# Modulating the two k-tiles of a pair on two engines, with a longer first piece of the split ahead and the masks cast in FFN 0

## The chip, the core and the metric

The kernel runs on one core of one Trainium2 chip. The core has five engines that each take their own queue of instructions in order and meet only through semaphores: TensorE (PE; its weight loads are shown as PEld), VectorE (DVE), ScalarE (ACT), GpSimd (POOL) and SyncE (SP), the last two issuing loads here. The metric is the device time of one launch in microseconds.

## What is computed

Two decoder layers over 256 tokens of width 1024, each with a half-step SwiGLU FFN, a token mixer and another FFN, every one modulated by shift, scale and gate rows computed from `c`, and closed by a residual with a LayerNorm. The reference, cut to what matters:

```python
D_MODEL = 1024; SEQ = 256; DEPTH = 2; N_HEADS = 8; D_FF = 2816
...
def layer_norm(x, g, b):
    xf = x.astype(jnp.float32)
    mu = jnp.mean(xf, axis=-1, keepdims=True)
    var = jnp.mean(jnp.square(xf - mu), axis=-1, keepdims=True)
    return ((xf - mu) * lax.rsqrt(var + LN_EPS) * g.astype(jnp.float32) + b.astype(jnp.float32)).astype(x.dtype)

def modulate(x, shift, scale):
    return x * (1.0 + scale[:, None, :]) + shift[:, None, :]

def post_norm_residual(x, y, gate, weight, g, b):
    return layer_norm(DEEPNORM_ALPHA * x + weight * (1.0 + gate[:, None, :]) * y, g, b)

def swiglu(h, w_in, w_out):
    g, u = jnp.split(h @ w_in, 2, axis=-1)
    return (jax.nn.silu(g) * u) @ w_out
...
    cond = jax.nn.silu(c)
...
    for l in range(DEPTH):
        if l == N_A_LAYERS:
            kv_mod = (cond @ w_kv_ada + b_kv_ada).reshape(b, 2, d)
            kv = modulate(x, kv_mod[:, 0], kv_mod[:, 1]) @ w_kv_b
...
        mod = (cond @ w_ada[l] + b_ada[l]).reshape(b, 3 * N_SUB, d)
        h = modulate(x, mod[:, 0], mod[:, 1])
        x = post_norm_residual(x, swiglu(h, w_ffn_in[l, 0], w_ffn_out[l, 0]), mod[:, 2], 0.5, ln_g[l, 0], ln_b[l, 0])
        h = modulate(x, mod[:, 3], mod[:, 4])
        if l < N_A_LAYERS:
            q, k, v = jnp.split(h @ w_qkv_a[l], 3, axis=-1)
...
            y = moba_attention(q, k, split_heads(v))
        else:
            q = split_heads(h @ w_q_b[l - N_A_LAYERS])
            y = stick_breaking_attention(q, k_sh, v_sh)
        y = merge_heads(y) @ w_o[l]
        x = post_norm_residual(x, y, mod[:, 5], 1.0, ln_g[l, 1], ln_b[l, 1])
        h = modulate(x, mod[:, 6], mod[:, 7])
        x = post_norm_residual(x, swiglu(h, w_ffn_in[l, 1], w_ffn_out[l, 1]), mod[:, 8], 0.5, ln_g[l, 2], ln_b[l, 2])
    return x
```

## The kernel before

All matrix products are done in three parts: a float32 weight `w` is split into `w_hi` (the value rounded to fp32r) and `w_lo = w - w_hi`, the activations likewise, and TensorE adds `hi*hi`, `lo*hi` and `hi*lo` into PSUM (lines 1460 to 1462 and 1556 to 1558 are the three matmuls of 128x512). Weights stream through five raw slots in chunks of 128 x 2048 elements (1 MB). SyncE loads a chunk (line 409), ScalarE writes `w_hi` (`split_hi`, line 586 for a whole chunk, 594 and 597 for one in two pieces), VectorE writes `w_lo` (`split_lo`, line 979) and with it frees the raw slot.

The tokens are two tiles of 128 (t = 0, 1), the width is eight k-tiles of 128 (k = 0 to 7). The order of all work on each engine is written out by hand; nothing is scheduled. Work runs as FFN 0, norm 0, projection and attention of layer 0, norm 1, FFN 1, norm 2, the shared keys and values (`KV_PAIRS`), FFN 2, norm 3, the queries of layer 1 (`Q_PAIRS`), stick-breaking attention, norm 4, FFN 3, last norm. After each of norms 0 to 4 stands the following input `h` in transposed form. What happens in one norm, for i = 0 to 4:

- VectorE (`norm`, line 1215): the residual of tile 0 in two halves (lines 1171, 1172), mean, normalising (1201); the first half of tile 1's residual; then `h_tile` of tile 0; then the second half of tile 1's residual, its mean and normalising; then `h_tile` of tile 1.
- ScalarE (`norm`, line 728): squares with sums (711) and the standard deviation (725) of tile 0; `h_tile` of tile 0; the first square of tile 1; the first 1024 columns of the split of the chunk ahead (594); the second square of tile 1, which waits for VectorE's residual; the deviation; a table load (739); `h_tile` of tile 1; the rest of the split (597).
- TensorE transposes the normalised tile in eight products (`turn_normed`, 1482). For tile 1 it does so inside `lead`, line 1588: 18 matmuls of tile 0 come first (k-tiles 0 to 5), then the eight transposes, then k-tiles 6 and 7, then tile 1 from k-tile 0 on.

`h_tile` works in halves of four k-tiles, each half in two pairs. A transposed k-tile lies in PSUM; modulating it (times `coef` scale, plus `coef` shift) gives `h_full` for tile 0 or `tmp` for tile 1; from it ScalarE writes `hT_hi` of a pair (697) and VectorE `hT_lo` of the pair (1151). In a half ScalarE modulates the first pair (691) and VectorE the second (1143). `h_hi` of the first pair waits for ScalarE's own semaphore `h_act`, that of the second for `h_dve`:

```python
def h_hi(i, t, pair):
    act.wait_ge(h_dve if pair % 2 else h_act, modulated(i, t, pair // 2))
```

`turn_place` says in which PSUM bank a transposed k-tile lies: the two tiles of a pair share a bank, so ScalarE and VectorE read from two different banks. The input of FFN 0 (i = 0) is made in the same way at the start, half by half, with the splits of chunks 1 and 2 after the first halves; that of FFN 2 (i = 4) is made among the projections of keys and values.

The three masks (identity, causal, strict) are cast to bf16 on VectorE (1322) just after norm 0 and used by the attention's scores. `quarter` inside `ffn` multiplies rows of `w_ada` by elements of the condition (1018, 1027) to make the modulation rows of later stages.

## Time and profile before

| | us |
|---|---|
| median of 3 runs | 1035.16 |
| lowest, highest of them | 1034.12, 1035.77 |
| the profiled execution | 1035.72 |
| its span | 1033.9 |
| TensorE busy | 1010.2 (98%) |
| VectorE busy | 788.1 (76%) |
| ScalarE busy | 529.3 (51%) |

The span reaches from the first to the last instruction of the profiled execution. The page's idle column puts down each idle stretch to the one that released it. A TensorE weight load is issued one matmul ahead, and matmul ends are modelled, so a stop of TensorE is best read from the starts of its matmuls, which stand 0.23 us apart at full clock.

### The profile page before, as it was taken

How to read it: one execution, taken by the hardware profiler on the slowest of the kernel's cores; microseconds unless marked ns; L12 is line 12 of the kernel's file. 1: busy time of each engine (PE TensorE's matmuls, PEld its weight loads, DVE VectorE, ACT ScalarE, POOL GpSimd, SP SyncE). 2: the span in 40 equal slices, each digit the busy share in tenths (PEclk: the TensorE clock that was granted, in tenths of full speed). 3: DMA queues.
4: the chain of work that ended last, by engine and by line, in shares of the span. 5: the costliest groups of instructions: out<-in, count | busy, mean ns of one | idle time of the engine just before them, and what ended most of it. 6: DMA issues, size and time to landing. Idle time of an engine off the chain costs nothing.

```text
span 1033.9 us, 12560 instructions
## 1 busy us (share of the span) xinstructions
PE 1010.2 (98%) x4768; PEld 834.0 (81%) x4768; DVE 788.1 (76%) x962; ACT 529.3 (51%) x872; POOL 86.0 (8%) x160
## 2 busy tenths in 40 slices
PE   4999999999999999999999999999999999999997
PEld 3878888887888888888888888888888888888885
DVE  6887677889877897768887587677888987545486
ACT  1635453566565753544474645453568764434433
POOL 0011111001000011112000011111001010000000
PEclk9999999999999999999999999999999999999999
DMA  9999999956785399899928499999846748556541
GB/s 353 376 380 359 303 299 313 320 163 203 255 274 163 129 377 346 294 315 305 332 101 295 142 358 301 308 304 311 302 161 207 242 141 306 185 183 204 174 151 41
DMA packets 147492, 265.63 MB, mean 257 GB/s; under 512 B 8424, under 2 KB 98920, under 8 KB 147432
## 3 DMA queue, kind: packets, MB, share of 16 engines
q1 hardware_dynamic: 124448, 182.87, 51.7%
q0 software_dynamic: 20928, 75.53, 20.9%
q10 hardware_dynamic: 2056, 6.42, 2.1%
q8 instruction: 38, 0.62, 0.2%
q14 instruction: 22, 0.18, 0.1%
HBM read 263.75 MB, written 1.05 MB: 256 GB/s over the span
## 4 chain that ended last, share of the span: by engine, by line
PE 89%; DVE 5%; ACT 2%; DMA 2%; issue 2%; SPq 0%; DVEq 0%; ACTq 0%
PE psum L1460 18%; PE psum L1462 18%; PE psum L1461 17%; PE psum L1556 9%; PE psum L1558 9%; PE psum L1557 9%; PE psum L1595 2%; DMA raw<-in_w_ffn_in 2%; DVE w_lo L979 2%; PE psum L1495 1%; ACT w_hi L586 1%; DVE tmp L1000 1%; PE psum L1861 1%; PE psum L1482 1%; PE psum L1692 1%
## 5 line engine op out<-in xcount | busy, mean ns | idle before, releaser
L979 DVE TENSOR_TENSOR w_lo<-raw,w_hi 128x2048 fp32r<-128x2048 f32 x164 | 371.6, 2287 | 61.7 <-ACT w_hi L586 59.5
L1460 PE MATMUL psum<-w_hi,hT_hi 128*128 128x512 f32 x896 | 355.9, 397 | 0.7 <-DVE w_lo L979 0.2
L1462 PE MATMUL psum<-w_hi,hT_lo 128*128 128x512 f32 x896 | 350.0, 391 | 0.0
L1461 PE MATMUL psum<-w_lo,hT_hi 128*128 128x512 f32 x896 | 349.0, 390 | 0.0
L586 ACT ACTIVATE w_hi<-raw 128x2048 fp32r<-128x2048 f32 x159 | 299.8, 1915 | 11.0 <-DMA raw<-in_w_ffn_in 9.5
L604 ACT ACTIVATE tmp<-psum 128x256 f32<-128x256 f32 x88 | 33.6, 383 | 338.3 <-PE psum L1462 338.3
L1460 PEld LDWEIGHTS psum<-w_hi,hT_hi 128*128 128x128 f32 x896 | 168.2, 188 | 36.7 <-issue 2.4
L1462 PEld LDWEIGHTS psum<-w_hi,hT_lo 128*128 128x128 f32 x896 | 168.2, 188 | 35.9
L1461 PEld LDWEIGHTS psum<-w_lo,hT_hi 128*128 128x128 f32 x896 | 168.5, 188 | 33.0
L1556 PE MATMUL psum<-w_hi,a_hi 128*128 128x512 f32 x368 | 148.5, 404 | 0.0
L1558 PE MATMUL psum<-w_hi,a_lo 128*128 128x512 f32 x368 | 144.3, 392 | 0.0
L1557 PE MATMUL psum<-w_lo,a_hi 128*128 128x512 f32 x368 | 144.2, 392 | 0.0
L1067 DVE TENSOR_TENSOR tmp<-psum,tmp 128x256 f32<-128x256 f32 x88 | 37.3, 424 | 119.7 <-ACT tmp L604 118.6
L1027 DVE SCALAR_TENSOR_TENSOR acc<-qT,cond,acc 128x1024 f32<-128x1024 f32 x64 | 82.0, 1281 | 3.3
L1027 DVE SCALAR_TENSOR_TENSOR acc<-ada,cond,acc 128x1024 f32<-128x1024 f32 x62 | 79.5, 1283 | 5.8 <-DMA ada<-in_w_ada 1.0
L1558 PEld LDWEIGHTS psum<-w_hi,a_lo 128*128 128x128 f32 x368 | 69.5, 189 | 15.0
L1557 PEld LDWEIGHTS psum<-w_lo,a_hi 128*128 128x128 f32 x368 | 69.7, 189 | 13.1
L1556 PEld LDWEIGHTS psum<-w_hi,a_hi 128*128 128x128 f32 x368 | 69.5, 189 | 13.3 <-issue 0.2
L507 POOL DMA_DIRECT2D ada<-in_w_ada x72 | 38.3, 532 | 410.4 <-DVE acc L1027 279.4
L507 POOL DMA_DIRECT2D qT<-in_w_ada x56 | 29.5, 528 | 292.4 <-DVE acc L1027 234.3
L1071 DVE TENSOR_TENSOR a_lo<-psum,a_hi 128x256 fp32r<-128x256 f32 x84 | 35.1, 418 | 7.3 <-ACT a_hi L608 7.3
L608 ACT ACTIVATE a_hi<-psum 128x256 fp32r<-128x256 f32 x84 | 31.9, 379 | 10.6 <-PE psum L1595 10.6
(171 smaller groups left out, 798.9 us busy)
## 6 DMA issues: line engine op xcount, KB each, us to landing
raw<-in_w_ffn_in SPq DMA_DIRECT2D x176, 512.0 KB, 5.6
raw<-in_w_ffn_out SPq DMA_DIRECT2D x88, 512.0 KB, 6.1
ada<-in_w_ada POOLq DMA_DIRECT2D x72, 512.0 KB, 6.1
qT<-in_w_ada POOLq DMA_DIRECT2D x56, 512.0 KB, 5.1
raw<-in_w_qkv_a SPq DMA_DIRECT2D x24, 512.0 KB, 4.7
raw<-in_w_o SPq DMA_DIRECT2D x16, 512.0 KB, 4.6
raw<-in_w_kv_b SPq DMA_DIRECT2D x16, 512.0 KB, 5.2
raw<-in_w_ada SPq DMA_DIRECT2D x4, 1024.0 KB, 16.3
```

Of the source, the lines that this page charges most:

```text
L507: pool.dma_start(ada_rows[place], ada_view(w)[:, row, j * D:(j + 1) * D])\
L586: nc.scalar.activation(hi_of(n), slot_of(n), ACT.Copy).then_inc(w_hi_ready, 1)
L979: nc.vector.tensor_tensor(lo_of(n), slot_of(n), hi_of(n).bitcast(F32), ALU.subtract)\
L1027: nc.vector.scalar_tensor_tensor(out=acc[:, :], in0=part, scalar=factor, in1=base, op0=ALU.mult, op1=ALU.add).then_inc(acc_steps, 1)
L1067: nc.vector.tensor_tensor(a_full[t], step_bank(f, s, t)[:, 256:512], silu_t[t], ALU.mult).then_inc(a_ready, 1)
L1071: nc.vector.tensor_tensor(inner_part(s, t, 1), inner_bank(f, s, t), inner_part(s, t, 0).bitcast(F32), ALU.subtract).then_inc(a_lo_ready, 1)
L1460: nc.tensor.matmul(dst, s_hi, m_hi, start=start, stop=False)
L1461: nc.tensor.matmul(dst, s_hi, m_lo, start=False, stop=False)
L1462: return nc.tensor.matmul(dst, s_lo, m_hi, start=False, stop=stop)
L1556: nc.tensor.matmul(dst, hi, m[0], start=first and j == 0, stop=False)
L1557: nc.tensor.matmul(dst, hi, m[1], start=False, stop=False)
L1558: end = nc.tensor.matmul(dst, lo, m[0], start=False, stop=last and j == 1)
```

## The change

1. A pair is modulated by both engines at once: ScalarE takes its even k-tile, VectorE its odd one, each with a semaphore step per tile. `h_hi` waits for both. ScalarE goes modulate, `h_hi`, modulate, `h_hi`; VectorE does its two tiles of a half, then `h_lo` of both pairs. `turn_place` puts the two tiles of a pair into two banks.
2. The first piece of the chunk ahead, which stands in front of the second square, has 1408 columns (`AHEAD`) in place of 1024.
3. In norms 0, 2 and 3 the rest of that split, 640 columns, is moved out of the norm to behind the copy of the first projected tile; in norms 1 and 4 it stays behind `h_tile`.
4. The masks are cast in FFN 0, after the last `split_lo` of step 4.

```diff
+AHEAD = 1408
...
+        def tiles_modulated(i, t, pair):
+
+            return 2 * modulated(i, t, pair // 2) - 1 + pair % 2
...
-            pair = k // 2
             if i in (0, 4):
-                bank, at = y[2 * (1 - t) + pair % 2], (k % 2 + 2 * (pair // 2)) * P
+                bank, at = y[2 * (1 - t) + k % 2], k // 2 * P
             else:
-                bank, at = ((misc + y[0:2]) if t == 0 else (y[2:4] + misc))[pair], (k % 2) * P
+                bank, at = ((misc + y[0:2]) if t == 0 else (y[2:4] + misc))[2 * (k // 4) + k % 2], (k % 4 // 2) * P
             return bank[:, at:at + P]
...
-            def h_pair(i, t, half):
-
-                act.wait_ge(turned, turned_count(i, t, half))
-                act.wait_ge(coef_ready, coef_count(i, half))
-                for k in (4 * half, 4 * half + 1):
-                    last = nc.scalar.activation(h_fulls[t][:, k, :], turn_place(i, t, k),
-                                                ACT.Identity, scale=coef[:, i, 0, k:k + 1], bias=coef[:, i, 1, k:k + 1])
-                last.then_inc(h_act, 1)
+            def modulate(i, t, pair):
+
+                act.wait_ge(turned, turned_count(i, t, pair // 2))
+                act.wait_ge(coef_ready, coef_count(i, pair // 2))
+                k = 2 * pair
+                nc.scalar.activation(h_fulls[t][:, k, :], turn_place(i, t, k), ACT.Identity,
+                                     scale=coef[:, i, 0, k:k + 1], bias=coef[:, i, 1, k:k + 1]).then_inc(h_act, 1)
 
             def h_hi(i, t, pair):
-                act.wait_ge(h_dve if pair % 2 else h_act, modulated(i, t, pair // 2))
+                act.wait_ge(h_act, tiles_modulated(i, t, pair))
+                act.wait_ge(h_dve, tiles_modulated(i, t, pair))
                 nc.scalar.activation(hT_hi[:, 2 * pair:2 * pair + 2, t * P:(t + 1) * P],
                                      h_fulls[t][:, 2 * pair:2 * pair + 2, :], ACT.Copy).then_inc(h_hi_ready, 1)
 
             def h_half(i, t, half):
-                h_pair(i, t, half)
-                h_hi(i, t, 2 * half)
-                h_hi(i, t, 2 * half + 1)
+                for pair in (2 * half, 2 * half + 1):
+                    modulate(i, t, pair)
+                    h_hi(i, t, pair)
...
                 deviation(i, 0)
                 h_tile(h, 0)
                 first_square(i, 1)
-                split_hi_first(ahead, CH // 2)
+                split_hi_first(ahead, AHEAD)
                 deviation(i, 1)
...
                 h_tile(h, 1)
-                split_hi_rest(ahead, CH // 2)
+                if i in (1, 4):
+                    split_hi_rest(ahead, AHEAD)
...
             keep_tile(q0, 0)
+            split_hi_rest(n + 2, AHEAD)
             split_hi(n + 3)
...
             keep_values(v0, 0, 0)
+            split_hi_rest(n + 2, AHEAD)
             split_hi(n + 3)
...
-            h_pair(4, 1, 0)
-            h_pair(4, 1, 1)
+            for pair in range(4):
+                modulate(4, 1, pair)
...
             keep_tile(q0, 0)
+            split_hi_rest(n + 2, AHEAD)
             split_hi(n + 3)
...
                     split_lo(n + 3 * s + 4)
+                    if (f, s) == (0, 4):
+                        dve.wait_ge(cst_in, 32)
+                        for m, mask in enumerate((ident, causal, strict)):
+                            last = nc.vector.tensor_copy(masks[:, m, :], mask)
+                        last.then_inc(masks_ready, 1)
...
-            def h_pair(i, t, half):
-
-                dve.wait_ge(turned, turned_count(i, t, half))
-                dve.wait_ge(coef_ready, coef_count(i, half))
-                for k in (4 * half + 2, 4 * half + 3):
-                    last = nc.vector.tensor_scalar(h_fulls[t][:, k, :], turn_place(i, t, k),
-                                                   coef[:, i, 0, k:k + 1], coef[:, i, 1, k:k + 1], ALU.mult, ALU.add)
-                last.then_inc(h_dve, 1)
+            def modulate(i, t, pair):
+
+                dve.wait_ge(turned, turned_count(i, t, pair // 2))
+                dve.wait_ge(coef_ready, coef_count(i, pair // 2))
+                k = 2 * pair + 1
+                nc.vector.tensor_scalar(h_fulls[t][:, k, :], turn_place(i, t, k), coef[:, i, 0, k:k + 1],
+                                        coef[:, i, 1, k:k + 1], ALU.mult, ALU.add).then_inc(h_dve, 1)
...
             def h_half(i, t, half):
-                h_pair(i, t, half)
+                modulate(i, t, 2 * half)
+                modulate(i, t, 2 * half + 1)
                 h_lo(i, t, 2 * half)
                 h_lo(i, t, 2 * half + 1)
...
             gate_unit = GATE_OF[1]
-            dve.wait_ge(cst_in, 32)
-            for m, mask in enumerate((ident, causal, strict)):
-                last = nc.vector.tensor_copy(masks[:, m, :], mask)
-            last.then_inc(masks_ready, 1)
             rope(q0, 0)
...
-            for half in range(2):
-                h_pair(4, 1, half)
+            for pair in range(4):
+                modulate(4, 1, pair)
```

Two places as the queues have them, and a third for the masks. First ScalarE in norm 0, from the start of `h_tile` of tile 0 to the second square of tile 1, before:

```order
L691 ACTIVATE h_full<-psum,coef 128x128 [waits coef_ready,turned]
L691 ACTIVATE h_full<-psum,coef 128x128
L697 ACTIVATE hT_hi<-h_full 128x2x128 [waits h_act]
L697 ACTIVATE hT_hi<-h_full 128x2x128 [waits h_dve]
...
L711 ACTIVATE psum,sq<-qT,first_mean 128x512 [waits first_mean_ready]
L594 ACTIVATE w_hi<-raw 128x1024 [waits w_used,raw_in0]
L711 ACTIVATE psum,sq<-qT,first_mean 128x512 [waits z_ends]
```

and after:

```order
L695 ACTIVATE h_full<-psum,coef 128x128 [waits coef_ready,turned]
L701 ACTIVATE hT_hi<-h_full 128x2x128 [waits h_dve,h_act]
L695 ACTIVATE h_full<-psum,coef 128x128 [waits coef_ready,turned]
L701 ACTIVATE hT_hi<-h_full 128x2x128 [waits h_dve,h_act]
...
L715 ACTIVATE psum,sq<-qT,first_mean 128x512 [waits first_mean_ready]
L598 ACTIVATE w_hi<-raw 128x1408 [waits w_used,raw_in0]
L715 ACTIVATE psum,sq<-qT,first_mean 128x512 [waits z_ends]
```

The first split of the half moved ahead of the second modulated tile, and each split waits for a tile of VectorE as well as for one of its own. The second half, left out in both, reads the same as the first.

Next ScalarE at the end of norm 3 and the start of the queries (`h_full` in L753 and L758 is the copy of the first projected tile), before:

```order
L697 ACTIVATE hT_hi<-tmp 128x2x128 [waits h_dve]
L597 ACTIVATE w_hi<-raw 128x1024
L753 ACTIVATE h_full<-psum 128x512 [waits first_tile]
L586 ACTIVATE w_hi<-raw 128x2048 [waits w_used,raw_in1]
L753 ACTIVATE h_full<-psum 128x512 [waits w_used]
```

and after:

```order
L701 ACTIVATE hT_hi<-tmp 128x2x128 [waits h_dve,h_act]
L758 ACTIVATE h_full<-psum 128x512 [waits first_tile]
L601 ACTIVATE w_hi<-raw 128x640
L590 ACTIVATE w_hi<-raw 128x2048 [waits w_used,raw_in1]
L758 ACTIVATE h_full<-psum 128x512 [waits w_used]
```

The copy moved ahead of the rest of the split.

Last VectorE in FFN 0, step 4 to 5, after the change; the two splits follow each other directly before it:

```order
L1035 SCALAR_TENSOR_TENSOR acc<-ada,cond,acc 128x1024 [waits acc_steps,ada_in1]
L987 TENSOR_TENSOR w_lo<-raw,w_hi 128x2048 [waits w_hi_ready]
L1135 CAST masks<-cst 128x128 [waits cst_in]
L1135 CAST masks<-cst 128x128 x2
L987 TENSOR_TENSOR w_lo<-raw,w_hi 128x2048 [waits w_hi_ready]
L1075 TENSOR_TENSOR tmp<-psum,tmp 128x256 [waits silu_ready]
```

The casts moved here from behind norm 0.

## Rows read from the trace of the kernel before

**Rows 1.** The page: TensorE's busy time, share of the span, number of instructions

```profile
PE 1010.2 (98%) x4768; PEld 834.0 (81%) x4768; DVE 788.1 (76%) x962; ACT 529.3 (51%) x872; POOL 86.0 (8%) x160
```

**Rows 2.** Waits of the weight loads: us in total, times, longest us

```profile
PEld psum L1460 <- issue: 2.4, 5, 0.5
PEld psum L1460 <- DVE w_lo L979: 1.2, 2, 0.7
```

**Rows 3.** Timeline of ScalarE in norm 0: start us, length us, engine, line, operation

```profile
226.25 0.81 ACT L691 ACTIVATE h_full<-psum,coef 128x128 f32<-128x128 f32 x2 [2.17 <-PE psum L1482]
...
230.11 1.04 ACT L594 ACTIVATE w_hi<-raw 128x1024 fp32r<-128x1024 f32 x1
231.56 0.69 ACT L711 ACTIVATE psum<-qT,first_mean 128x512 f32<-128x512 f32 x1 [0.41 <-DVE qT L1172]
...
234.63 0.81 ACT L691 ACTIVATE tmp<-psum,coef 128x128 f32<-128x128 f32 x2 [0.62 <-PE psum L1482]
235.47 0.73 ACT L697 ACTIVATE hT_hi<-tmp 128x256 fp32r<-128x256 f32 x2
```

**Rows 4.** Timeline of VectorE in norm 0

```profile
226.77 0.73 DVE L1143 TENSOR_SCALAR h_full<-psum,coef 128x128 f32<-128x128 f32 x2
...
230.10 0.69 DVE L1171 TENSOR_TENSOR qT<-psum,gate 128x512 f32<-128x512 f32 x1
...
232.94 1.00 DVE L1201 TENSOR_SCALAR qT<-qT,nmean,rstd 128x512 f32<-128x512 f32 x2
234.63 0.73 DVE L1143 TENSOR_SCALAR tmp<-psum,coef 128x128 f32<-128x128 f32 x2 [0.69 <-PE psum L1482]
235.92 0.76 DVE L1151 TENSOR_TENSOR hT_lo<-tmp,hT_hi 128x256 fp32r<-128x256 f32 x2 [0.56 <-ACT hT_hi L697]
```

**Rows 5.** Timeline of TensorE in norm 0 and the projection behind it

```profile
233.99 1.04 PE L1482 MATMUL psum<-cst,qT 128*128 128x128 f32 x8
...
235.79 0.39 PE L1461 MATMUL psum<-w_lo,hT_hi 128*128 128x512 f32 x1
236.02 0.40 PE L1462 MATMUL psum<-w_hi,hT_lo 128*128 128x512 f32 x1
236.49 0.48 PE L1460 MATMUL psum<-w_hi,hT_hi 128*128 128x512 f32 x1
...
245.72 0.50 PE L1460 MATMUL psum<-w_hi,hT_hi 128*128 128x512 f32 x1 [0.25 <-DVE w_lo L979]
```

**Rows 6.** Timeline of three engines at the start of the queries

```profile
778.85 1.05 ACT L597 ACTIVATE w_hi<-raw 128x1024 fp32r<-128x1024 f32 x1
779.80 0.58 ACT L753 ACTIVATE h_full<-psum 128x512 f32<-128x512 f32 x1
779.92 2.29 DVE L979 TENSOR_TENSOR w_lo<-raw,w_hi 128x2048 fp32r<-128x2048 f32 x1 [0.53 <-ACT w_hi L597]
780.27 1.90 ACT L586 ACTIVATE w_hi<-raw 128x2048 fp32r<-128x2048 f32 x1
...
784.72 2.29 DVE L979 TENSOR_TENSOR w_lo<-raw,w_hi 128x2048 fp32r<-128x2048 f32 x1
...
787.06 0.49 PE L1460 MATMUL psum<-w_hi,hT_hi 128*128 128x512 f32 x1
```

**Rows 7.** Timeline of VectorE in FFN 0, and the casts after norm 0

```profile
125.65 0.42 DVE L1067 TENSOR_TENSOR tmp<-psum,tmp 128x256 f32<-128x256 f32 x1 [2.37 <-ACT tmp L604]
...
238.15 0.49 DVE L1322 CAST masks<-cst 128x128 bf16<-128x128 f32 x3
```

**Rows 8.** The chain of work that ended last, at the start: start us, us, what

```profile
40.83 13.66 DMA raw<-in_w_ffn_in
```

**Rows 9.** Timeline of TensorE in FFN 0: its idle before this transpose

```profile
59.74 0.44 PE L1595 MATMUL psum<-cst,tmp 128*128 128x128 f32 x2 [1.85 <-DVE tmp L1067]
```

**Rows 10.** Windows: us, busy (count) of PE, PEld, DVE, ACT, POOL; granted clock, DMA, GB/s

```profile
60.00:62.00 2.00, 2.00 (x7) 1.49 (x6) 2.00 (x5) 1.79 (x2) 0.00 (x0) 0.56 1.10 349
62.00:64.00 2.00, 2.00 (x7) 1.57 (x6) 2.00 (x2) 0.89 (x2) 0.00 (x0) 0.59 1.11 349
```

## The prediction

> **What bounds the kernel now.** First the page: TensorE (PE) is busy 1010.2 of 1033.9 us [rows 1], so another engine matters only where TensorE waits for it. Next the waits of its weight loads [rows 2]: after the start there are only five stops before a matmul of line 1460, 2.4 us in sum, and two stops for `w_lo`, 1.2 us in sum. These rows overstate the loss, since a weight load goes one matmul ahead. What is lost shows in the starts: two matmuls in a row start 0.23 us apart (235.79, 236.02), the next one 0.47 us later, at 236.49 [rows 5]. So a stop costs 0.24 us and five cost 1.2 us. They stand where the second token tile of each norm reaches TensorE; the matmul needs the first pair of `hT_lo`, which VectorE works on from 235.92 and ends at about 236.35 [rows 4]. The two `w_lo` stops cost less than their 1.2 us, some 0.7. All that the norms and what follows them can give back is thus about 1.9 us, 0.18%. A measurement of this kernel can tell about 0.2%, 2.1 us, from no change.
>
> **Part 1: the pairs, second tile.** Both engines start at 234.63 [rows 3, 4]. Before, ScalarE modulates k-tiles 0 and 1 in 0.81 us (two of 0.45 with 0.1 of overlap) and starts `hT_hi` of pair 0 at 235.47 [rows 3]. After, ScalarE does k-tile 0 while VectorE does k-tile 1, so `hT_hi` starts at 235.11, 0.36 us earlier, and `hT_lo` of the pair ends at 236.0. The stop of 0.24 us would go: five norms, -1.2 us.
>
> **Part 2: the pairs, first tile.** Here the two don't start together: ScalarE at 226.25 [rows 3], VectorE at 226.77 [rows 4], because the residual of the second tile's first half stands ahead of it. Before, only the second `hT_hi` of a half needs VectorE. After, every one does, and VectorE still makes `hT_lo` of pairs 0 and 1 ahead of its k-tiles 5 and 7. So pair 2 goes round both engines: `hT_hi` 1, `hT_lo` 1, k-tile 5, `hT_hi` 2. I stepped both queues with the rows' durations (modulate 0.45 and 0.41, split 0.42 and 0.43, 0.03 us from an end to the start of what needs it, 0.1 us of overlap where nothing is needed). So stepped, the old order gives the trace's times within 0.05 us. The new order lets VectorE go on to the last residual at 230.8, where it starts at 230.10 now [rows 4]: 0.7 us later.
>
> **Part 3: 1408 columns.** 1024 columns take 1.04 us, and ScalarE then idles 0.41 us until the residual is done [rows 3]; 2048 take 1.90 us [rows 6]. A column costs 0.84 ns, so 1408 take 1.37 us. By part 2 ScalarE starts this piece 0.8 us late and is free at 232.33, the residual ends at 232.24: the longer piece itself costs 0.1 us. Second square, standard deviation and normalising are then 0.77 us late. TensorE begins the transposes at 233.99 [rows 5] and needs only the first half of the normalised tile, ready at about 233.5 (the two halves run from 232.94 to 233.94) [rows 4]: 0.5 us of room. Of 0.77 us, 0.3 is left as a new stop ahead of the transposes. In norms 1 and 4, where VectorE starts its first tile later still against ScalarE, the stepping gives 0.66 late and 0.2 of stop. With the transposes later the second tile's `hT_lo` lands at its old time, and TensorE, later too, doesn't wait for it. So the stop moves: parts 1 to 3 together give 0.3 - 0.24, about +0.1 us for norms 0, 2 and 3 and 0 for norms 1 and 4.
>
> **Part 4: where the rest of the split stands.** The second tile lasts 0.6 us longer on both engines (each pair is again a chain over both) and starts 0.3 us later, so ScalarE is through with it 0.9 us later. In norms 1 and 4 the rest of the split shrinks from 1.05 us [rows 6] to 0.72 (640 columns) and stays where it is; `w_lo` and the gated product behind it come 0.5 us late, within TensorE's room there: 0. In the others a tile copy of 0.58 us [rows 6] now stands ahead of the rest.
> - Norm 0: the copy starts when it did, RoPE follows it and not the rest, and both `w_lo` keep their times. The stop before 245.72 [rows 5] stays and swallows this norm's 0.1 us: 0.
> - Norm 2 (keys and values): `w_lo` 1.0 us late, with about that much room. From 0 to 0.3; I take 0.15, and with the norm's own 0.1: +0.25.
> - Norm 3 (queries): VectorE runs without a break from `w_lo` at 779.92 over two gate products to the second `w_lo`, 784.72 to 787.0, and TensorE starts at 787.06 behind it [rows 6]. That stretch begins when the rest ends, 778.85 + 1.05 = 779.9. Now ScalarE is free at 779.7, copies until 780.3 and ends the rest at 780.92. All moves by 1.03 us, with TensorE waiting for its end: **+1.05 us**, this norm's own stop included.
>
> **Part 5: the masks.** The three casts, 0.49 us, leave the projection, where they lay beside the wait for a tile copy, for FFN 0, where VectorE idles 2.37 us before its next gated product [rows 7]: 0 and 0.
>
> **Part 6: the start.** In the first half tiles the chain over both engines costs ScalarE 0.6 us, so `w_lo` of chunks 1 and 2, and the load that the first frees, come about 0.55 us later. That load takes 13.66 us from issue to landing [rows 8], which is a queue and not its own transfer. TensorE has 1.85 us of idle behind it [rows 9]. I take 0 and keep 0.55 for the range.
>
> **Sum.** 0 + 0 + 0.25 + 1.05 + 0 = +1.3 us. On the profiled execution (1035.72 us, of which 1033.9 are its span) that gives 1037.0; it lay 0.56 us above the median of the runs shown, so against the median 1036.4.
>
> **The rivals.**
> - *The room before the transposes hides the first tile.* If the first tile's lateness stays under 0.5 us, nothing stops the transposes and part 1's 0.24 us stands in norms 1, 2 and 4 (norm 0's goes into its `w_lo` wait): -0.7. If the queries' stretch, too, isn't later, their norm's 0.24 us goes as well: -1.0, 1034.2. With that stretch late by 0.9 the sum is +0.2, 1035.4. For it: the room is real. Against: VectorE starts half a microsecond after ScalarE, by the program's order. Chance 0.12 for 1034.2 and 0.13 for 1035.4.
> - *The half clock at the start (the slower side).* The granted clock is 0.56 in the 2 us from 60 and 0.59 in the next 2 [rows 10], right behind TensorE's 1.85 us of idle [rows 9]; before and after it is full. At half clock (1.2 GHz for 2.4) this loses 2 x 0.44 + 2 x 0.41 = 1.7 us. The later chunks 1 and 2 make a break or two in TensorE's work shortly before. If these or a longer idle bring a second such stretch, 1036.4 + 1.7 = 1038.1; it decides from where chunk 1 or 2 comes later than TensorE's room, about 0.3 us for chunk 1. Chance 0.13. A shorter idle without the stretch would give 1034.7: 0.05.
>  The Trainium skill (TensorE: Matmul & The Clock Gate, What's actually happening) says that the gate is released by activity and that its phase is independent of the program's start. The trace agrees on the first; no row shows the second.
> - *The load follows its issue.* The 0.55 us of part 6 reach TensorE: 1037.0. Chance 0.07.
> - *The change does more than remove stops.* Above 0.2% needs the start's idle to shrink besides all the norms' stops: 1032.9. Chance 0.05.
>
> The forecast as worked out has the remaining 0.45.
>
> **How the numbers follow.** Likeliest: 1036.4. 1034.2 less a few tenths for the spread of three runs gives the low end, 1033.9; the high end, 1038.0, stands just short of the clock's 1038.1 and holds the queue's 1037.0 and norm 2's 0.15. Left out are the gain of 0.05 and most of the clock's 0.13. Within 0.2% is 1033.1 to 1037.2. Slower by more: the clock's 0.13 and a part of the forecast's upper side, 0.19. Faster by more: 0.07. The rest is 0.74.
>
> **What would show it.** Right: the second tile's first matmul 0.23 us behind the one ahead; a stop of 0.2 to 0.3 us before the transposes of the second tile; the second square some 0.75 us later against the first tile's start; the queries' second `w_lo` about 1 us later against the matmuls of their norm, and TensorE right behind it. Wrong: `hT_hi` of the first tile's first pairs not held by VectorE, transposes without a stop, or a queries' stretch that starts no later.

## The result, and the profile after

The changed kernel takes 1037.38 us (median of 9 runs, 1036.96 to 1039.46) where the kernel before, run beside it, takes 1034.12 us (9 runs, 1033.85 to 1035.77): slower by 3.3 us (the medians' quotient is 1.0032; the recorded ratio is 1.0026, with 1.0017 to 1.0035 as its interval). The forecast was 1036.4 us, 1.3 us slower, with 1033.9 to 1038.0 as the range. So the time lay in the range, but the likeliest case had been "within 0.2%", and the loss is two and a half times the one worked out (about twice by the recorded ratio). The profiled execution of after took 1037.43 us, 1035.6 of which are its span.

The executions of the kernel before, here and in the batches below, fall into two groups, at 1033.8 to 1034.7 and 1035.1 to 1036.5 us; two of the three that the prediction had lie in the upper one, and so does its profile (1035.72 us).

The page of after has the same busy times as [rows 1] within 0.2 us on TensorE and VectorE; all of the loss is waiting:

```profile
PE 1010.1 (98%) x4768; PEld 832.2 (80%) x4768; DVE 788.2 (76%) x962; ACT 529.5 (51%) x872; POOL 85.2 (8%) x160
```

The waits of its weight loads answer [rows 2] (us in total, times, longest us). L1469 is the matmul that was L1460, L1491 the transposes of a norm (1482 before), L1604 the transposes of an FFN's product (1595 before):

```profile
PEld psum L1491 <- DVE qT L1214: 3.2, 5, 0.7
...
PEld psum L1469 <- DVE w_lo L987: 3.0, 3, 1.2
PEld psum L1469 <- issue: 1.4, 3, 0.5
PEld psum L1604 <- DVE tmp L1075: 1.4, 3, 0.8
```

Five waits before the transposes are new, the two for `w_lo` have become three, and the five short ones of the second tiles are gone; the three short ones here stand elsewhere (at 41 us, in the keys and values at 544, in the queries at 784). Norm 0 shows the first. ScalarE, against [rows 3]:

```profile
224.85 0.46 ACT L695 ACTIVATE h_full<-psum,coef 128x128 f32<-128x128 f32 x1 [2.21 <-PE psum L1491]
225.82 0.42 ACT L701 ACTIVATE hT_hi<-h_full 128x256 fp32r<-128x256 f32 x1 [0.52 <-DVE h_full L1156]
...
227.91 0.42 ACT L701 ACTIVATE hT_hi<-h_full 128x256 fp32r<-128x256 f32 x1 [0.53 <-DVE h_full L1156]
...
229.74 1.37 ACT L598 ACTIVATE w_hi<-raw 128x1408 fp32r<-128x1408 f32 x1
231.01 0.66 ACT L715 ACTIVATE psum<-qT,first_mean 128x512 f32<-128x512 f32 x1
```

VectorE, against [rows 4]:

```profile
225.32 0.73 DVE L1156 TENSOR_SCALAR h_full<-psum,coef 128x128 f32<-128x128 f32 x2
226.27 0.43 DVE L1163 TENSOR_TENSOR hT_lo<-h_full,hT_hi 128x256 fp32r<-128x256 f32 x1 [0.23 <-ACT hT_hi L701]
...
229.50 0.68 DVE L1184 TENSOR_TENSOR qT<-psum,gate 128x512 f32<-128x512 f32 x1
...
232.37 1.02 DVE L1214 TENSOR_SCALAR qT<-qT,nmean,rstd 128x512 f32<-128x512 f32 x2
```

TensorE, against [rows 5]:

```profile
232.37 0.39 PE L1471 MATMUL psum<-w_hi,hT_lo 128*128 128x512 f32 x1
232.97 1.13 PE L1491 MATMUL psum<-cst,qT 128*128 128x128 f32 x8 [0.21 <-DVE qT L1214]
233.85 0.47 PE L1469 MATMUL psum<-w_hi,hT_hi 128*128 128x512 f32 x1
...
235.08 0.40 PE L1471 MATMUL psum<-w_hi,hT_lo 128*128 128x512 f32 x1
235.32 0.39 PE L1469 MATMUL psum<-w_hi,hT_hi 128*128 128x512 f32 x1
```

Read in this order: ScalarE waits 0.52 and 0.53 us for VectorE's k-tile before two of its four `hT_hi`; its second square starts 6.16 us after its first modulate (224.85 to 231.01) where it was 5.31 us (226.25 to 231.56); VectorE normalises 7.52 us after that modulate (6.69 before); and TensorE's transposes start 0.60 us behind the matmul ahead of them, where matmuls in a row are 0.23 apart. The stop of the second tile is gone: 235.08 to 235.32 is 0.24 us, where [rows 5] has 0.47.

To see where the 3.2 us arise, each matmul of after was set against the same matmul of before in the two profiled executions, since TensorE runs the same 4768 in the same order. The shift (start in after less start in before) moves almost only in steps; a few hundredths of drift between two steps are counted with the nearer one:

| place | what makes the step | step, us | predicted |
|---|---|---|---|
| start and FFN 0, up to 59.9 | +0.17 before 31, stops of +0.30 at 41 and +0.91 at 47 (chunks 1 and 2 late), then 1.26 less idle at 59.9 | +0.17 | 0 |
| norm 0 | transposes +0.45, second tile -0.32 | +0.14 | +0.1, swallowed later |
| attention, 287 | one transposition late | +0.15 | 0 |
| norm 1 | the same two | +0.13 | 0 |
| FFN 1, 352 and 363 | first transposes +0.10, the next ones +0.54 | +0.64 | 0 |
| norm 2 | the same two | +0.20 | +0.1 |
| keys and values, 544 | `w_lo` later | +0.33 | +0.15 |
| norm 3 | the same two | +0.16 | in the next line |
| queries, 784 and 788.5 | `w_lo` +0.37, second `w_lo` +0.75 | +1.12 | +1.05 |
| norm 4 and FFN 3 | the same two +0.08, first transposes +0.10 | +0.18 | 0 |
| sum | | +3.2 | +1.3 |

The two spans differ by only 1.7 us, since before's profiled execution also lost 1.6 us at half clock [rows 10], and after's has none there (last section).

The largest step that the prediction did not have is at 363 in FFN 1. VectorE and then TensorE of after there:

```profile
348.38 2.29 DVE L987 TENSOR_TENSOR w_lo<-raw,w_hi 128x2048 fp32r<-128x2048 f32 x1 [0.20 <-ACT w_hi L601]
...
362.52 0.42 DVE L1075 TENSOR_TENSOR tmp<-psum,tmp 128x256 f32<-128x256 f32 x1
```

```profile
362.30 0.39 PE L1471 MATMUL psum<-w_hi,hT_lo 128*128 128x512 f32 x1
363.08 0.41 PE L1604 MATMUL psum<-cst,tmp 128*128 128x128 f32 x2 [0.40 <-DVE tmp L1075]
```

And TensorE of before at the same transposes:

```profile
363.15 0.39 PE L1462 MATMUL psum<-w_hi,hT_lo 128*128 128x512 f32 x1
363.42 0.41 PE L1595 MATMUL psum<-cst,tmp 128*128 128x128 f32 x2
```

From the first `w_lo` behind norm 1 VectorE has no idle time for 14.5 us, until the product that these transposes need. Nor had it any in before, where the same row reads:

```profile
348.71 2.29 DVE L979 TENSOR_TENSOR w_lo<-raw,w_hi 128x2048 fp32r<-128x2048 f32 x1 [0.53 <-ACT w_hi L597]
...
362.86 0.42 DVE L1067 TENSOR_TENSOR tmp<-psum,tmp 128x256 f32<-128x256 f32 x1
```

There it ended just in time (at 363.28, and 0.27 us lie between the starts of matmul and transposes). That `w_lo` starts 0.33 us earlier in after (348.38 against 348.71), but the matmuls are 0.88 us earlier by then, so it is 0.55 us late against TensorE, and nearly all of the 0.55 arrives 14 us later.

The queries, against [rows 6]: ScalarE, VectorE, TensorE of after.

```profile
779.85 0.42 ACT L701 ACTIVATE hT_hi<-tmp 128x256 fp32r<-128x256 f32 x1
780.17 0.58 ACT L758 ACTIVATE h_full<-psum 128x512 f32<-128x512 f32 x1
780.65 0.73 ACT L601 ACTIVATE w_hi<-raw 128x640 fp32r<-128x640 f32 x1
```

```profile
781.41 2.29 DVE L987 TENSOR_TENSOR w_lo<-raw,w_hi 128x2048 fp32r<-128x2048 f32 x1 [0.69 <-ACT w_hi L601]
...
786.20 2.29 DVE L987 TENSOR_TENSOR w_lo<-raw,w_hi 128x2048 fp32r<-128x2048 f32 x1
```

```profile
787.33 0.40 PE L1471 MATMUL psum<-w_hi,hT_lo 128*128 128x512 f32 x1
788.54 0.49 PE L1469 MATMUL psum<-w_hi,hT_hi 128*128 128x512 f32 x1 [0.81 <-DVE w_lo L987]
```

The stretch on VectorE starts 1.49 us later than the 779.92 of before (0.20 of it is the shift that after had by then), and TensorE starts 788.54 right behind its end. This is the part that went as forecast.

### The profile page after: what moved, and what is told of

Same layout as the page of the kernel before. It is cut to its first block, busy times and chain, and to the rows that moved or that the text cites. A ratio compares the mean times of both kernels' runs of the same rounds, so it can differ in the third digit from the quotient of the medians.

```text
span 1035.6 us, 12672 instructions
## 1 busy us (share of the span) xinstructions
PE 1010.1 (98%) x4768; PEld 832.2 (80%) x4768; DVE 788.2 (76%) x962; ACT 529.5 (51%) x872; POOL 85.2 (8%) x160
## 3 DMA queue, kind: packets, MB, share of 16 engines
HBM read 263.75 MB, written 1.05 MB: 256 GB/s over the span
## 4 chain that ended last, share of the span: by engine, by line
PE 80%; DVE 10%; ACT 5%; issue 3%; DMA 2%; SPq 0%; DVEq 0%; ACTq 0%
PE psum L1469 16%; PE psum L1471 16%; PE psum L1470 16%; PE psum L1565 8%; PE psum L1567 8%; PE psum L1566 8%; DVE w_lo L987 3%; DMA raw<-in_w_ffn_in 2%; PE psum L1604 2%; ACT w_hi L590 2%; PE psum L1504 1%; ACT psum L715 1%; DVE tmp L1008 1%; DVE qT L1185 1%; PE psum L1870 1%
## 5 line engine op out<-in xcount | busy, mean ns | idle before, releaser
L1469 PE MATMUL psum<-w_hi,hT_hi 128*128 128x512 f32 x896 | 356.0, 397 | 2.0 <-DVE w_lo L987 1.7
L1469 PEld LDWEIGHTS psum<-w_hi,hT_hi 128*128 128x128 f32 x896 | 168.2, 188 | 38.0 <-DVE w_lo L987 3.0
```

Source lines behind the costliest of these rows:

```text
L1469: nc.tensor.matmul(dst, s_hi, m_hi, start=start, stop=False)
```

## The experiments

Three batches, each against the kernel before on the same chip: its medians there were 1034.13, 1034.37 and 1034.54 us (27, 33 and 27 runs). The ratios are against those. "Against after" compares with 1037.38, which was measured in none of these batches. Kernels with the same start differ by up to 0.4 us at 59.9 us of their profiles, so differences of 0.3 us in the times stand for nothing; the steps inside a profile are read finer.

### The pairs alone, and everything but the pairs

`e1_pairs_only`: before, with the new pairs everywhere; 1024 columns, the rest in every norm, the masks as they were.

```
-AHEAD = 1408
+AHEAD = 1024
-                if i in (1, 4):
+                if i in (0, 1, 2, 3, 4):
                     split_hi_rest(ahead, AHEAD)
```

(The edit is shown against after; left out of it are the three later `split_hi_rest`, which are gone, and the masks, which are back.)

> The kernel before with the new pairs alone (both engines on each pair, in every tile); 1024 columns ahead, the rest of the split at the end of each norm, masks after norm 0. Theory (the first tile's chain over both engines makes the second tile late): transposes of the second tile stop TensorE by 0.2 to 0.3 us in each norm, the stop before the second tile's first matmul is gone, ScalarE leaves the norm 0.9 us late with a rest of 1.05 us behind it, so the stop in FFN 1 and the one at the queries' second chunk are there as well: +2.5 to +3.3 us against before. Rival (the longer piece and the moved rest do the harm, the pairs alone gain): -1 to +0.5 us.

1038.19 us, ratio 1.0038 (1.0025 to 1.005): +4.1 us, more than the 2.5 to 3.3 expected. Its profile has the expected steps before the transposes, in FFN 1 and in the queries, and one that was not expected, +0.93 against before, in the first projection:

```profile
241.82 0.47 PE L1465 MATMUL psum<-w_hi,hT_hi 128*128 128x512 f32 x1 [0.77 <-DVE w_lo L984]
```

The `w_lo` there stands behind RoPE (the rotation of queries and keys) on VectorE, and RoPE behind ScalarE's copy, which in this kernel waits for the rest of the split. `e2_all_but_pairs` keeps the other parts and has the old `h_pair` and `turn_place`:

```
-                for pair in (2 * half, 2 * half + 1):
-                    modulate(i, t, pair)
-                    h_hi(i, t, pair)
+                h_pair(i, t, half)
+                h_hi(i, t, 2 * half)
+                h_hi(i, t, 2 * half + 1)
```

> The changed kernel with the old pairs (each engine its own pair of a half): 1408 columns ahead, rest of the split behind the first projected copy in norms 0, 2 and 3, masks in FFN 0. Theory: ScalarE idles 0.41 us before the second square, 384 columns more cost 0.33 us of it, and the copy ahead of the rest costs the queries 0.16 us: 0 to +0.3 us against before, the five stops before the second tile as before. Rival (the longer piece and the moved rest do the harm): +2 us or more.

1033.5 us, 0.9994 (0.9985 to 1.0003): -0.6 us where 0 to +0.3 was expected; the interval holds 1. So the pairs are the whole loss and more, and the columns, the place of the rest and the masks give back a little (e1 to after: -0.8; before to e2: -0.6). In e2 the five stops at the second tiles are as before, and the `w_lo` stop of [rows 5] at 245.72 is gone (a step of -0.52): that is the gain of the rest behind the copy. A second step, -0.25 before the transposes of `acc` at 380, isn't explained by any run; in the queries e2 loses 0.15.

### Which pairs

`e3_second_tile_only` has the new pairs only in the second tile of each norm, with 1408 columns, the rest in every norm and the masks as in after. Shown is the condition alone; the old `h_pair` and `turn_place`, which hold wherever it is false, are left out here and in the variants below:

```
+        def both(i, t, half):
+            return t == 1 and i not in (0, 4)
```

> New pairs in the second tile of each norm alone, old pairs in the first tile and at the start; 1408 columns ahead, the rest of the split inside every norm, masks in FFN 0. Theory: the first tile ends on time, so the transposes don't stop and the five stops of 0.24 us go; ScalarE is 0.6 us longer in the second tile, 0.33 of it given back by the shorter rest, so the queries' stretch is 0.3 us late: -1.0 to -0.2 us against before. Rival (the waits between the engines cost as much in the second tile): 0 to +1 us.

1034.97 us, 1.0008 (0.9999 to 1.0017): +0.8, where I had expected a gain of 0.2 to 1.0; the rival named there (0 to +1) fits. Its profile has neither the transposes' stop nor the second tile's. It has others, behind the second tile; TensorE at the first one:

```profile
239.87 0.40 PE L1512 MATMUL psum<-w_hi,hT_lo 128*128 128x512 f32 x1
240.10 0.60 PE L1726 MATMUL psum<-cst,h_full 128*128 128x128 f32 x4
241.21 0.47 PE L1510 MATMUL psum<-w_hi,hT_hi 128*128 128x512 f32 x1 [0.51 <-DVE w_lo L1013]
```

Against before this is a step of +0.67, with +0.50 at 362.54 and +0.64 at 786.22: each time a `w_lo` or a product at the end of an unbroken row on VectorE that began with the end of the second tile. The chain over both engines makes the second tile longer, and that is paid behind the norm, in three places. Only the first half needs to be quick, so `e4_first_half_of_second_tile` has the new pairs in half 0 alone:

```
-            return t == 1 and i not in (0, 4)
+            return t == 1 and half == 0 and i not in (0, 4)
```

> As the kernel with new pairs in the second tile alone, but only in its first half (pairs 0 and 1); its second half and the first tile have the old pairs. Theory: the first hT_lo comes 0.36 us earlier as TensorE wants it, and ScalarE leaves the tile only 0.15 us later, less than the 0.33 us that the shorter rest gives back: the five stops go, the stop at the queries' second chunk shrinks by 0.1 to 0.2 us: -1.5 to -0.9 us against before, the fastest of the four. Rival: as fast as the kernel with the whole second tile.

1033.07 us, 0.9989 (0.998 to 0.9998): -1.1 us. In its profile all five stops of the second tile are gone, in steps of -0.32 or -0.33 (sum -1.6), and the three places of e3 are late again, but only by +0.13, +0.14 and +0.13 (at 242.51, 363.29 and 786.37). The net is that of part 1 of the prediction, priced there at -1.2; it agrees because a larger gain and a cost that part 1 did not have nearly make up for each other.

### The first tile

`e6_vector_modulates_first`: after, but in tile 0 of each norm VectorE does its four k-tiles before any `hT_lo`.

```
+                if t == 0 and i not in (0, 4):
+                    for pair in range(4):
+                        modulate(i, t, pair)
+                    for pair in range(4):
+                        h_lo(i, t, pair)
+                    return
```

> The changed kernel, but in the first tile of each norm VectorE modulates all its four k-tiles before it makes any hT_lo. Theory (pair 2 goes round both engines): ScalarE waits for VectorE at the first pair alone, the second square comes 0.35 to 0.4 us earlier, and of the lateness less than the 0.5 us of room is left, so the stops before the transposes go or fall under 0.1 us: -1.0 to -1.5 us against the changed kernel, +1.8 to +2.3 against before. Rival (the lateness is that of the first pair, or of the 1408 columns): -0.3 to 0 against the changed kernel.

1035.19 us, 1.0007 (0.9998 to 1.0015): -2.2 us against after, more than the 1.0 to 1.5 expected. VectorE, ScalarE and TensorE in norm 0:

```profile
225.22 1.36 DVE L1156 TENSOR_SCALAR h_full<-psum,coef 128x128 f32<-128x128 f32 x4
```

```profile
229.14 1.37 ACT L598 ACTIVATE w_hi<-raw 128x1408 fp32r<-128x1408 f32 x1
230.41 0.67 ACT L715 ACTIVATE psum<-qT,first_mean 128x512 f32<-128x512 f32 x1
```

```profile
232.21 0.39 PE L1477 MATMUL psum<-w_hi,hT_lo 128*128 128x512 f32 x1
232.44 1.06 PE L1497 MATMUL psum<-cst,qT 128*128 128x128 f32 x8
```

The second square comes 5.70 us after the first modulate (224.71), and all five stops before the transposes are gone, each step between -0.40 and -0.52, in sum -2.3 (its start gives another 0.15 and a few hundredths come back between the norms). So the round over both engines (`hT_hi` 1, `hT_lo` 1, k-tile 5, `hT_hi` 2) is what made the first tile late enough to stop TensorE: with `hT_lo` out of it and the pairs unchanged, 0.46 of the second square's 0.85 us go, and the 0.39 that is left stops nothing. The stops behind the second tile stay, at 543, 362 and 786.70 us.

### The columns and the rest

`e12_1024_columns` is after with `AHEAD = 1024`.

> The changed kernel with 1024 columns ahead in place of 1408, all else as changed. Theory (the longer piece costs the second square 0.1 us at most and spares 0.33 us behind the norms): stops before the transposes 0.1 us shorter, the stop in FFN 1 and those for w_lo behind norms 2 and 3 up to 0.33 us longer: +0.2 to +0.8 us against the changed kernel, +3.5 to +4.1 against before. Rival (the 1408 columns make the second square late): -1 us against the changed kernel.

1038.48 us, 1.004 (1.0028 to 1.0053): +1.1 us against after, a little over the upper end of what was expected (0.8), and +3.9 against before, within it. ScalarE in norm 0, and TensorE in FFN 1:

```profile
229.41 1.04 ACT L598 ACTIVATE w_hi<-raw 128x1024 fp32r<-128x1024 f32 x1
230.62 0.69 ACT L715 ACTIVATE psum<-qT,first_mean 128x512 f32<-128x512 f32 x1 [0.17 <-DVE qT L1185]
```

```profile
351.12 0.44 PE L1604 MATMUL psum<-cst,tmp 128*128 128x128 f32 x2 [0.19 <-DVE tmp L1075]
```

With 1024 columns the second square comes 6.15 us after the first modulate (224.47), with 1408 6.16: the first waits 0.17 us for VectorE's residual, the second starts behind the split with no wait, and the split and the residual end within 0.2 us of each other (231.11 and 230.92 in after). So in norm 0 the longer piece costs nothing ahead of the transposes. In the other norms it costs a little: the starts of matmul and transposes are 0.03, 0.10, 0.04 and 0.03 us farther apart in after than here. Its worth lies behind the norm, where the rest is 0.73 us and not 1.04: the profile of 1024 has steps of +0.18 at 241, +0.33 at 351, +0.33 at 544, +0.34 at 784 and +0.30 at 853 against after.

`e7_rest_in_norm` is after with the rest in every norm:

```
-                if i in (1, 4):
+                if i in (0, 1, 2, 3, 4):
```

> The changed kernel with the rest of the split (640 columns) inside every norm, ahead of the copy of the first projected tile. Theory: the queries' stretch starts 0.5 us earlier (-0.5), keys and values -0.2, but in norm 0 copy and RoPE and with them the w_lo behind them come 0.6 us later (+0.6): -0.3 to +0.1 us against the changed kernel, the three parts to be seen one by one in the trace. Rival (the copy ahead of the rest causes the queries' stop): -1.0 us, the stop at the queries' second chunk gone.

1036.99 us, 1.0022 (1.0013 to 1.0031): -0.4 against after, at the edge of what was expected; its start alone makes up as much (its profile is 0.40 us ahead at 59.9). Inside, the move of the rest shows with both signs: without it a stop of +0.64 appears at 241.47 (the first projection's `w_lo`, as in e3), while 0.35 at 544, 0.37 at 784 and 0.15 at 788 go. Moving the rest behind the copy pays 0.64 us in norm 0 and costs 0.35 and 0.52 in norms 2 and 3.

### The queries' row of VectorE

`e8_splits_first_in_queries`: after, both `w_lo` ahead of the gate products.

```
             split_lo(n + 2)
-            accumulate(gate_unit, 0)
             split_lo(n + 3)
+            accumulate(gate_unit, 0)
```

> The changed kernel with one line moved: in the queries VectorE makes both w_lo before the two gate products. Theory: the stop before the queries' second chunk, 0.98 us by the starts, is VectorE's unbroken stretch; with 2.6 us of products out of it the stop is gone: -0.8 to -1.0 us against the changed kernel. Rival (the stop is given back in the attention, whose queues are late anyway): -0.2 to 0 us.

1036.73 us, 1.0021 (1.0012 to 1.003): -0.65 against after, between the theory (-0.8 to -1.0) and the rival (-0.2 to 0); some 0.2 of it is this profile's start. VectorE, and TensorE at the first scores:

```profile
781.22 4.49 DVE L987 TENSOR_TENSOR w_lo<-raw,w_hi 128x2048 fp32r<-128x2048 f32 x2 [0.69 <-ACT w_hi L601]
```

```profile
790.61 0.70 PE L1859 MATMUL psum<-qT,kT 128*128 128x256 f32 x2 [0.35 <-ACT qT L762]
```

TensorE gains 1.1 us at 788.5, and loses 0.6 again at the scores, which wait for ScalarE's `qT`; the likely reason is that the products now stand ahead of the row that the queries' scaling needs, which no run separates. Half of the stop was order; the other half is not got rid of by order, since VectorE begins as late as before the edit (781.22 here, 781.41 in after, 0.2 of it the start).

### The start

`e5_start_only`: before, with the new pairs only in the first transposed input.

```
+        def both(i, t, half):
+            return i == 0
```

> The kernel before with the new pairs in the first FFN's input alone. Theory (the start costs little by itself): ScalarE's start is 0.55 us longer, TensorE stops for chunks 1 and 2 by up to 1 us in sum, and the idle before the transposes of FFN 0 shrinks by as much, so 0 to +0.3 us against before among executions of the same clock; since the long idle is broken up, fewer executions have the half-clock stretch of 1.7 us. Rival (the delay passes through the load): +0.5 us or more.

1034.24 us, 0.9997 (0.9988 to 1.0006), lowest 1033.72 against 1033.79 of before. Its profile has steps of +0.32 us at 41.07 and +0.90 at 47.40, and gives both back at 59.26, where TensorE waits 0.17 us, not 1.85. So the start costs nothing, as forecast.

### Putting the useful parts together

`e9_first_half_rest_behind_copy` has the old pairs with the new ones in half 0 of the second tiles, 1408 columns, the rest and the masks as in after. `e10_and_the_start` adds the new pairs at i = 0, `e11_and_the_queries` adds the order of e8.

```
 e9:         return t == 1 and half == 0 and i not in (0, 4)
 e10, e11:   return (t == 1 and half == 0 and i not in (0, 4)) or i == 0
```

> New pairs in the first half of each norm's second tile alone; 1408 columns, masks in FFN 0, and the rest of the split behind the first projected copy in norms 0, 2 and 3 as in the changed kernel. Theory (the parts add up: all but the pairs gave -0.6, the five stops are worth 1.2): the stop before the first projection's second w_lo stays away, the queries' stop grows by 0.3 us: -1.9 to -1.3 us against before. Rival (moved rest and earlier pairs get in each other's way): -1.1 us or less gain.

1032.7 us, 0.9986 (0.9977 to 0.9995): -1.8 us.

> As the kernel with new pairs in the first half of the second tile and the rest behind the copy, with the new pairs at the start as well. Theory: the start by itself costs 0 to 0.2 us, but it breaks up TensorE's idle of 1.85 us in FFN 0, so the half-clock stretch of 1.7 us falls away in nearly all executions: the lowest times as without it or 0.2 above, the median at or under the one without, hardly any execution more than 1 us above the lowest. Rival (the stretch comes by chance whatever the idle is): a third of the executions 1.5 us above the others, as before.

1032.74 us, 0.9982 (0.9973 to 0.9991): -1.8 us.

> As the kernel with the start added, and both w_lo of the queries ahead of the two gate products on VectorE. Theory: the stop before the queries' second chunk (0.4 to 0.6 us in this kernel) goes; part of it comes back in front of the first scores, as in the changed kernel with that order, where 0.5 of 1.0 us came back: -0.2 to -0.5 us against the same kernel without it.

1032.3 us, 0.9976 (0.9967 to 0.9985): -2.2 us against before and -5.1 against after; the fastest of all. The median of the kernel before is 0.4 us higher in this batch than in the first, which adds to these three gains: by the lowest times (1034.03 for before; 1032.51, 1032.53 and 1032.08) they are 1.5, 1.5 and 1.95 us.

In e10 three of 11 executions lie 1 us or more above the lowest, in e9 four of 11. That is not the "hardly any" that was expected of e10, and nearer to its rival; the median is the same.

By the lowest times e9, with the rest behind the copy, gains 0.4 us more than e4, with the rest in the norm, and by the profiles 0.1: the stop at 245 goes (a step of -0.40), as in e2, and the queries pay as much back. With only half of the second tile lengthened the rest comes early enough there, and the cost that after had at 544 and 784 isn't seen. At 786.25 e9 has a step of +0.59 (the queries' second `w_lo`; +0.13 in e4), which e11 takes away; e11 waits at the scores instead (0.59 us between two starts that are 0.23 apart in e10).

## Why the prediction was right in kind and short in size

**Right: which stops go and which come.** Second tile's first matmul 0.24 us behind the one ahead (forecast 0.23); a new stop before the transposes in all five norms; the second square 0.85 us later against the first modulate (forecast 0.75); `hT_hi` held by VectorE; the queries' stretch later, with TensorE right behind. e6 shows the cause of the stop before the transposes, e1 and e2 that the pairs make the whole loss. That e4 comes out at -1.1 where part 1 had -1.2 is luck in the size: five stops were worth 1.6, and 0.4 was lost again behind them.

**Parts 1 to 3, the net of a norm.** Forecast +0.1 in norms 0, 2 and 3 and 0 in 1 and 4. Measured +0.14, +0.20, +0.16 and +0.13, +0.08: 0.7 in sum, not 0.3. The stop before the transposes was mis-sized: 0.31 to 0.44 us and 0.09 more inside the transposes behind it, where the sum had 0.3 and 0.2. The gain at the second tile was mis-sized too, the other way: each stop costs 0.24 us and then 0.08 up to the matmul after it. In norm 0 the step that failed was "the stop before 245.72 stays and swallows this norm's 0.1 us". It stayed and swallowed nothing, since VectorE's `w_lo` there comes out of the same lateness.

**Part 4, norms 1 and 4.** The step that failed is "`w_lo` and the gated product behind it come 0.5 us late, within TensorE's room there: 0". The 0.5 was right (0.55). The room was read at the wrong place: at the first transposes behind the norm, which lose only 0.10, and not at the end of VectorE's unbroken row, 14.5 us on, where before had 0.27 us between two starts and so no room at all. This is 0.64 us, the largest miss, and it is the same pattern that part 4 had found in the queries and priced there. It had been looked for only where a stop already stood.

**Part 4, norms 2 and 3.** Keys and values +0.33 against 0.15, queries with their norm +1.28 against 1.05. The direction and the mechanism held; in the queries the first `w_lo` (+0.37 at 784) stopped TensorE as well. The mis-sized term is ScalarE's lateness at the end of the second tile: its copy starts at 780.17, where 779.7 was forecast; less the 0.18 that after was late by then, this is 1.14 us late and not 0.85. The second tile is 0.6 us longer, as forecast, but starts 0.5 later (the stop and what it costs inside the transposes) and not 0.3. e7 shows that moving the rest is a loss of 0.35 and 0.52 at these two places, the direction that part 4 had, but a gain of 0.64 at 241, which I had not seen: with the pairs in the whole second tile, RoPE's inputs come late there.

**Part 3, the columns.** "The longer piece itself costs 0.1 us": it costs 0.01 in norm 0 and 0.2 over the other four norms, and its gain behind the norms, 1.5 us by e12, had been left out, as a gain of its own; it stood inside the lateness of part 4 (a rest of 0.72 us and not 1.05), so the sum didn't suffer.

**Parts 5 and 6.** The masks cost nothing that a profile shows, except that a transposition of the attention starts 0.83 us behind the work ahead of it (0.68 before), a step of +0.15; e1, which leaves the masks where they were, has the same step, so it isn't theirs. It is there in every kernel with the new pairs in the first tile of the norms and in none of the others; how it comes about stays open. The start was 0.17 in this profile and 0 by e5, but not as part 6 had it: chunks 1 and 2 stop TensorE by 1.2 us in sum, where 0.55 was named, and TensorE's idle time of 1.85 us takes all of it.

**The base.** The forecast stood at 1035.16, the median of three, and the true median of the kernel before is 1034.1 to 1034.5. From 1034.1 the same sum would have given 1035.4, 2 us short of the result, and a range moved along with it would have ended at about 1036.9, below the 1037.38. That the time fell in the range is that luck.

**The rivals.** Room before the transposes did not hide the first tile: no. The load follows its issue: no (e5). The second half-clock stretch at the start: no, the one that was there became rarer (next section). A gain above 0.2%: not in after; e11 has it, by other edits.

## What to carry to other kernels

When work is split more finely over two engines, step both queues to the end of the row without idle time, not only to the first consumer: what is late by half a microsecond at the row's start is late by the same at its end, and the consumer there may have had no room, without showing any stop before the change. A hand-over for every piece shortens the time to the first piece and lengthens the time to the last one; use it for the piece that somebody waits for (the first half of the second tile, -1.1 us), not for all (+4.1 us). And where an engine serves two chains, put the operations that the other engine waits for ahead of those that only a later consumer needs (e6, -2.2 us for one change of order).

## What the runs showed of the hardware

**A stop costs more than its idle time.** TensorE's starts are 0.23 us apart. Where the operand came a little late, at each of the five second tiles of before, the next start was 0.47 us on, and the one after it 0.31 or 0.32 and not 0.23 (236.02, 236.49, 236.81): 0.32 us in all, for an operand that landed at about 236.35 where the matmul was due at 236.25 [rows 4, 5]. After a stop before the transposes, the eight of them take 0.87 or 0.88 us to the next matmul in after, and not the 0.79 of before.

**Half clock after a long stop, sometimes.** In before's profile the granted clock is 0.56 and 0.59 in the four microseconds behind 1.85 us of idle time [rows 9, 10]; that is the 1.2 GHz level for part of it. TensorE of after at the same place, and its windows (us, busy and counts, granted clock):

```profile
59.90 0.44 PE L1604 MATMUL psum<-cst,tmp 128*128 128x128 f32 x2 [0.59 <-DVE tmp L1075]
```

```profile
60.00:62.00 2.00, 2.00 (x9) 1.53 (x10) 2.00 (x5) 1.62 (x2) 0.00 (x0) 1.00 1.06 366
62.00:64.00 2.00, 2.00 (x10) 1.67 (x9) 2.00 (x2) 1.02 (x2) 0.00 (x0) 1.00 1.10 346
```

The clock is full and 19 matmuls fit where 14 did. But the same idle time doesn't always bring it. e3 waits 1.78 us there and keeps its clock:

```profile
59.67 0.44 PE L1645 MATMUL psum<-cst,tmp 128*128 128x128 f32 x2 [1.78 <-DVE tmp L1101]
```

```profile
60.00:62.00 2.00, 2.00 (x9) 1.61 (x9) 2.00 (x4) 1.86 (x2) 0.00 (x0) 1.00 1.10 350
```

Of the fourteen profiled executions, the five that took more than 1 us over their kernel's lowest time (before, e2, e4, e9, e10) have a stretch of half clock between 32 and 1020 us, and the nine others none. Over all runs, of the kernels with the old start 51 of 140 executions lie more than 1 us above the lowest of their kernel in that batch, of those with the new start (0 to 0.7 us of idle in their profiles) 11 of 85. So such executions are rarer with the new start. That the shorter idle time is the reason is the likely reading; e9 and e10, which differ in the start alone, have four and three of 11 and don't show it. Nor does the new start exclude them: the profile of e10 has half clock elsewhere. Its TensorE idles 1.62 us before 31.29, where the `zeros` matmuls ended early (in after's profile they reach to 31.27), and the windows from 34 us on read (us, busy and counts, granted clock):

```profile
34.00:36.00 2.00, 2.00 (x12) 2.00 (x12) 1.41 (x5) 1.44 (x5) 0.00 (x0) 0.50 1.10 348
36.00:38.00 2.00, 2.00 (x10) 1.55 (x11) 1.05 (x4) 1.97 (x4) 0.00 (x0) 0.50 1.10 349
```

The profiles of e2, e3, e4, e7, e8 and e12 have 1.6 us of idle time there too, and full clock right behind it (30 to 40 us).

The Trainium skill (TensorE: Matmul & The Clock Gate, What's actually happening) says that the gate's phase is independent of the program's start. e3 against before, with nearly the same idle time and two outcomes, agrees with that, and so do these seven at 31 us. So does the stretch of half clock that every profile has between 20 and 32 us: in the three stretches of 4 us there the granted clock is 0.85, 0.50 and 0.80 in after and 0.99, 0.58 and 1.00 in e8, which is the same program up to the queries. No run here sets the phase and so shows it.
